# Three selected pages loaded early, turns woven with scores, and an output projection from three rounded products

## The chip, the cores and the metric

The kernel runs on one core of one Trainium2 chip, as one launch. The metric is the device time of that launch in microseconds (us), the median of several runs. The core's engines are TensorE (PE; its weight loads are listed as PEld), VectorE (DVE), ScalarE (ACT), GpSimd (POOL) and SyncE (SP, which issues most of the transfers). They run their own instruction streams and wait for each other through semaphores.

## The reference, cut to what matters

One inference step of one decoder layer, in float32, for a prompt of 1024 tokens and for 8 sample sequences of one token each with a past of 2048 tokens in pages of 128.

```python
h = x @ w_in                      # q | compressed k,v | selected k,v | window k,v | gates | HGRN2 parts | merge gates
a = NSA(h)                        # compressed blocks + selected top-16 blocks + sliding window, ALiBi
r = HGRN2(h)                      # gated linear recurrence
merged = sigmoid(g_a) * (a @ w_br_a) + sigmoid(g_r) * (r @ w_br_b)
mix = merged @ w_out              # (tokens, 1024) @ (1024, 1024): the output projection
x1 = LN(alpha * x + mix)
y = LN(alpha * x1 + relu(x1 @ w_up)**2 @ w_down)
```

For the sample sequences, the compressed branch turns all 16 pages of each sequence's `cache_cmp_kv` into block keys and values, and the selected branch attends to the 16 best of 33 blocks of `cache_sel_kv`:

```python
past_c = cache_cmp[page_table]                 # (8, 2048, 2, 2, 64)
kv_cmp = blocks_from_parts(chunk_parts(past_c, cmp_w), cmp_w, cmp_pos)
o_c, p_c = compressed_branch(q, pos_q, kv_cmp, slopes)
idx, valid = select_blocks(p_c, pos_q, n_sel)
o_s = selected_branch(q, pos_q, cache_sel[blocks idx], idx, valid, slopes)
```

## The kernel before

All orders are written out by hand: each engine has one program, and semaphores tie them together. Nearly all on-chip memory is one tensor, `arena`, that the phases cut up anew; `PS` is PSUM, eight banks of 512 floats. The phases follow each other: attention projections, prompt attention, sample attention (454 to 660 us of the profile), HGRN2 with its projections, merge, output projection with the first LayerNorm, then `up` and `down` of the MLP, and the second LayerNorm.

**Sample attention.** A "page" of this stage is a half: the 128 rows of 8 tokens that one half of each of a sequence's 16 pages gives, 1 MB in one indirect load by POOL (L2580), 128 partitions of 2048 floats. There are 16 for the compressed branch (n = 0 to 15) and 16 for the selected one (m = 0 to 15; sequence `m % 8`, half `m // 8`). Both use the two buffers of `raw` in turn. POOL issues load n when PE has turned load n-2 (`d_ps`), and from the third selected one on also when ACT has copied its values (`v_s`).

For a compressed page PE turns 16 blocks of 128x128 (`cmp_turn`, L1108), DVE and ACT copy them out of PSUM, and PE multiplies the previous page's by the compression weights (`cmp_products`, L1123). For a selected page m, `sel_turn` (L1147) turns the page's keys in two halves of four blocks, one PSUM bank each (4 and 5); ACT copies the values into `vall` (L1677) and then the first half of the turned keys into `ktd` (L1681), DVE copies the second half (L2152). `sel_scores` (L1156) multiplies the queries of the sequence by each half and adds up in banks 0 to 3. The two are called in turn: all of a page's turns, then all of its scores. `vall` has a place of 2048 floats for each sequence's values; those of sequences 5, 6 and 7 are first written by pages 5, 6 and 7. Between pages DVE also does the softmax of the compressed scores (L2096 on), the importance and rank of the blocks (L2110 to L2126), and after page 15 the maximum over the selected scores (L2141 on).

**Merge.** For 8 groups of 128 output channels and 3 chunks of 344 tokens, 24 steps s: PE makes two gates in split form and two plain products (L1407), ACT the sigmoids (L1764), DVE two products and their sum into `mT` (L2353, L2354), which frees the step (`m_dve2`).

**Split form.** Where the kernel calls `split_product` (L818), a float32 product is made from three products of rounded operands (`F32R`): high x high, high x low and low x high. The high part is a copy into an `F32R` tensor (ACT, L836 for weights), the low part is the value minus the high part (DVE, L842 for weights). A plain product of float32 operands shows as two records in the trace.

**Output projection.** `mT` holds the merged activations, 8 k-tiles of 128 channels x 1032 tokens; `wo` holds `w_out`, whose k-tiles 4 to 7 are loaded during the merge and 0 to 3 (L778) when the gates of the last step are done. PE goes through `LN_ORDER` = tile 0, the 8 sample rows (position p = 1), then tiles 1 to 7:

```python
for part in (1, 0):
    if p == 0:
        pe.wait_ge(wo_in[part], 16)
    for half in range(2):
        for k in range(4 * part, 4 * part + 4):
            mm = pe.matmul(PS[:, 2 * (p % 2) + half, :], mT[:, k, P * t:P * t + P],
                           wo[:, k, 512 * half:512 * (half + 1)], start=(k == 4), stop=(k == 3))
```

That is 16 plain products of 512 columns a tile (L1434). The sample rows take 16 products with 8 columns of weights, packed four at a time into strips of the array (L1440). After each tile DVE adds the residual (L2392, for the sample rows L2397 and L2402), takes the statistics and norms the tile (L2362 to L2369); PE turns the normed tile one position later (`turn_x1`, L1421), ACT copies the high part to `x1h` (L1809) and DVE makes the low part `xl` (L2378). `x1h` lies in the same place as `mT`. SP loads the two LayerNorm rows (L782, L783) and the residual rows (L788) behind eight `w_up` loads. `up` follows (L818 again), and then `down`, 512 columns a product, in split form.

## Time before, and what its profile page says

| what | us |
|---|---|
| median of the timed runs | 2204.72 |
| lowest and highest of the 3 | 2200.83, 2205.96 |
| the profiled execution | 2196.05 |
| its span, first to last instruction | 2194.2 |
| PE busy | 2118.1 |
| DVE busy | 1020.0 |
| ACT busy | 689.5 |
| POOL busy | 162.4 |

Busy times are the union of an engine's instructions in the profiled execution. The span is what the profile covers, and the execution's own time has a little around it. Matmuls are pipelined, so the duration of a record is longer than its distance from the next one; what a product costs is read from the distance. The mean granted PE clock is 0.99 of full speed.

### The profile page before, as it was taken

The numbers are of one execution on the slowest core, as the hardware profiler recorded it, in microseconds if no ns is written. First come the engines' busy times: TensorE is split into PE (matmuls) and PEld (weight loads), VectorE is DVE, ScalarE is ACT, GpSimd is POOL, SyncE is SP. The second block draws the span as 40 slices with busy tenths as digits, with TensorE's granted clock in tenths as the row PEclk, the third lists the DMA queues.
The fourth block names the chain that finished last, engine by engine and source line by source line (L and its number), as shares of the span: only waits on it lengthen the run. The fifth ranks groups of instructions, "written<-read, shape, count | busy, mean of one in ns | idle before, by whom it ended". The sixth has DMA issues, their size and how long they took to land.

```text
span 2194.2 us, 33354 instructions
## 1 busy us (share of the span) xinstructions
PE 2118.1 (97%) x14090; PEld 1800.0 (82%) x14090; DVE 1020.0 (46%) x1872; ACT 689.5 (31%) x1342; POOL 162.4 (7%) x164
## 2 busy tenths in 40 slices
PE   8999999989889999999999999999999999999997
PEld 8997777759659999999888884479888998889985
DVE  2136666636532666766212114544444444444447
ACT  3227777734432444544111110122211122111222
POOL 0030000001110221311000000000000000000007
PEclk9999999989999999999999999999999999999999
DMA  9322000146672221213212113021111111111101
GB/s 235 99 79 96 11 11 1 50 146 207 204 236 78 61 58 45 69 45 89 86 30 57 30 60 105 29 80 46 48 39 44 54 49 49 39 39 58 39 20 78
DMA packets 140625, 158.90 MB, mean 72 GB/s; under 512 B 25842, under 2 KB 122315, under 8 KB 135612
## 3 DMA queue, kind: packets, MB, share of 16 engines
q1 hardware_dynamic: 132444, 113.98, 17.3%
q0 software_dynamic: 8032, 42.78, 6.3%
q8 instruction: 112, 1.84, 0.3%
q14 instruction: 37, 0.30, 0.0%
HBM read 141.16 MB, written 19.76 MB: 73 GB/s over the span
## 4 chain that ended last, share of the span: by engine, by line
PE 90%; DVE 3%; DMA 3%; ACT 2%; issue 1%; SPq 0%; DVEq 0%; ACTq 0%; POOLq 0%
PE PS L818 58%; PE PS L1434 5%; PE PS L1407 5%; PE PS L1040 3%; PE PS L1123 3%; PE PS L1020 2%; DMA arena<-in_cache_sel_kv,arena 2%; PE PS L992 2%; PE PS L994 1%; PE PS L1108 1%; PE PS L1333 1%; PE PS L1476 1%; PE PS L1049 1%; PE PS L1276 1%; PE PS L1219 1%
## 5 line engine op out<-in xcount | busy, mean ns | idle before, releaser
L818 PE MATMUL PS<-x_low,w_high_mlp 128*128 128x344 f32 x1056 | 337.7, 320 | 0.0
L818 PE MATMUL PS<-w_down_high,hidden 128*128 128x512 f32 x960 | 308.1, 395 | 0.9 <-DVE w_down_low L2468 0.9
L818 PE MATMUL PS<-x_high,w_low 128*128 128x344 f32 x768 | 245.8, 320 | 0.0
L2462 DVE TENSOR_TENSOR arena<-arena,PS 128x512 f32<-128x512 f32 x244 | 167.5, 687 | 134.9 <-PE PS L818 134.7
L818 PE MATMUL PS<-x_high,w_high_mlp 128*128 128x344 f32 x720 | 229.8, 319 | 0.0
L818 PEld LDWEIGHTS PS<-w_down_high,hidden 128*128 128x128 f32 x960 | 180.1, 188 | 54.2 <-DVE arena L2462 12.0
L818 PE MATMUL PS<-w_down_low,hidden 128*128 128x512 f32 x512 | 201.0, 392 | 0.0
L818 PEld LDWEIGHTS PS<-x_low,w_high_mlp 128*128 128x128 f32 x1056 | 198.2, 188 | 2.5
L818 PE MATMUL PS<-x_low,w_high_hgrn 128*128 128x344 f32 x600 | 192.5, 321 | 0.0
L818 PE MATMUL PS<-x_high_a,w_low 128*128 128x344 f32 x480 | 154.1, 321 | 0.0
L818 PE MATMUL PS<-x_high_b,w_low 128*128 128x344 f32 x468 | 149.6, 320 | 0.0
L818 PEld LDWEIGHTS PS<-x_high,w_low 128*128 128x128 f32 x768 | 144.2, 188 | 0.0
L818 PEld LDWEIGHTS PS<-x_high,w_high_mlp 128*128 128x128 f32 x720 | 135.4, 188 | 1.5 <-issue 0.9
L1537 ACT ACTIVATE arena<-PS 128x344 f32<-128x344 f32 (+1 forms) x105 | 47.9, 458 | 262.6 <-PE PS L818 262.4
L1407 PE MATMUL PS<-arena,wring 128*128 128x344 f32 x384 | 114.7, 452 | 1.2 <-issue 1.2
L1836 ACT ACTIVATE w_down_high<-arena 128x2048 fp32r<-128x2048 f32 x15 | 28.7, 1916 | 275.2 <-PE PS L818 275.2
L1434 PE MATMUL PS<-arena 128*128 128x512 f32 x256 | 112.9, 599 | 1.8 <-DVE arena L2354 1.8
L818 PEld LDWEIGHTS PS<-x_low,w_high_hgrn 128*128 128x128 f32 x600 | 113.7, 189 | 0.0
L818 PEld LDWEIGHTS PS<-w_down_low,hidden 128*128 128x128 f32 x512 | 96.1, 188 | 21.2
L842 DVE TENSOR_TENSOR w_low<-wring,w_high_mlp 128x1024 fp32r<-128x1024 f32 x44 | 53.6, 1221 | 109.7 <-ACT w_high_mlp L836 109.7
L818 PE MATMUL PS<-x_high_a,w_high_hgrn 128*128 128x344 f32 x300 | 101.9, 340 | 1.5 <-DMA x_high_b<-x_high_kept 1.5
L2622 POOL TENSOR_TENSOR arena<-arena 128x1024 f32<-128x1024 f32 (+1 forms) x8 | 19.6, 2450 | 1119.1 <-ACT arena L1848 1119.1
(369 smaller groups left out, 4126.8 us busy)
## 6 DMA issues: line engine op xcount, KB each, us to landing
wring<-in_w_in SPq DMA_DIRECT2D x100, 256.0 KB, 3.4
wring<-in_w_up SPq DMA_DIRECT2D x64, 256.0 KB, 3.3
arena<-in_w_down SPq DMA_DIRECT2D x16, 1024.0 KB, 5.0
arena<-in_x_prompt SPq DMA_DIRECT2D x16, 512.0 KB, 3.8
x_high_kept<-x_high_att SPq DMA_DIRECT2D x1, 4128.0 KB, 14.3
arena<-in_cache_win_kv SPq DMA_DIRECT2D x8, 512.0 KB, 4.8
arena<-in_w_out SPq DMA_DIRECT2D x2, 2048.0 KB, 8.8
out<-in_cache_win_kv SPq DMA_DIRECT2D x1, 4088.0 KB
```

Of the source, the lines that this page charges most:

```text
L818: mm = pe.matmul(out, w, x, start=(start and k == 0 and i == 0), stop=(stop and k == tiles - 1 and i == 2))
L842: dve.tensor_tensor(wl[:, n % WR, :, 0:m], wring[:, n % WR, :, 0:m], high[:, :, 0:m].bitcast(F32), ALU.subtract).then_inc(wl_dve, 1)
L992: pe.matmul(out, qa, k1[g][:, br, k0:k0 + n], start=True, stop=False)
L994: mm = pe.matmul(out, qb, k2[br][g][0:65, k0:k0 + n], start=False, stop=True)
L1020: mm = pe.transpose(PS[0:n, 4 + turned % 2, P * b:P * (b + 1)], probs(j, col, n), ident)
L1040: mm = pe.matmul(PS[HD * two:HD * (two + 1), 6 + i % 2, c:c + P], v[0:r, :], PT[(2 * n + two) % 3][0:r, b // 4, P * (b % 4):P * (b % 4 + 1 ...
L1123: mm = pe.matmul(PS[:, 4 + 2 * (b % 2) + c, 0:256], cw2[:, c, 4 * half + q, :], xt2[:, n % 2, 256 * (4 * c + q):256 * (4 * c + q + 1)], st ...
L1407: mm = pe.matmul(PS[:, product_bank(s, ab), 0:cn], wring[:, n % WR, 4 * ab + k, :], a[:, k, c0:c0 + cn], start=(k == 0), stop=(k == 3))
L1434: mm = pe.matmul(PS[:, 2 * (p % 2) + half, :], mT[:, k, P * t:P * t + P], wo[:, k, 512 * half:512 * (half + 1)], start=(k == 4), stop=(k = ...
L1537: act.activation(dst[0:m, c0:c0 + cn], unit_out(3 * n + ci, m, cn), fn).then_inc(u_act, 1)
L1836: act.activation(wdh[:, :, :], wdn[:, g % 2], ACT.Copy).then_inc(wdh_act, 1)
L2462: dve.tensor_tensor(y, y, PS[:, 5 + d % 3, :], ALU.add).then_inc(dn_dve, 1)
```

## The change

1. **Loads.** The first three selected pages (`AHEAD = 3`) are loaded into the places of `vall` for sequences 5, 6 and 7, each issued right behind compressed page 4, 8 or 12. The other 13 use the two buffers of `raw` in turn, as before; the first two of them are issued when compressed pages 14 and 15 have been turned.
2. **Woven turns.** PE turns a half of page m+1, then multiplies the same half of page m, and so on.
3. **Projection.** Tiles 1 to 7 use the split form for k = 0 to 6 and a plain product for k = 7. Tile 0 uses the split form for k = 4, 5, 6 and plain products for the rest, and so do the sample rows. High parts of the activations go to `xl`, low parts over `mT` itself; high parts of the weights go to the room of the constants and of `aT`, low parts over `wo` itself. PE starts tile 0 before the last merge sum.

```diff
+        AHEAD = 3
+
+        def selected_raw(m):
+            if m < AHEAD:
+                b = NB - AHEAD + m
+                return vall[:, b, :, :].rearrange("p l c -> p (l c)")
+            return raw[:, (m - AHEAD) % 2, :]
+
+        def selected_in(m):
+            if m < AHEAD:
+                return ((kv_out[0], KV_ALL[0] + 16), (kv_out[1], KV_ALL[1] + 16), (vd_out, 16))[m]
+            return raw_in[(m - AHEAD) % 2], 16 * (8 + (m - AHEAD) // 2 + 1)
...
+        def out_high(k):
+            return wohK[:, k - 4] if k >= 4 else woha[:, k]
+        def mixed(p):
+            n = toks(LN_ORDER[p])
+            return (slice(None), slice(4, 7) if p < 2 else slice(0, 7), slice(P * LN_ORDER[p], P * LN_ORDER[p] + n))
...
# PE, selected pages
-            for m in range(16):
-                sel_turn(16 + m)
-                sel_scores(m)
+            for s in range(2):
+                sel_turn(0, s)
+            for m in range(16):
+                for s in range(2):
+                    if m + 1 < 16:
+                        sel_turn(m + 1, s)
+                    sel_scores(m, s)
...
# PE, projection
-            pe.wait_ge(m_dve2, NM)
+            pe.wait_ge(m_dve2, NM - 1)
...
+                pe.wait_ge(ul_dve, p + 1)
+                if p == 0:
+                    pe.wait_ge(wl_dve, SPLITS_O + 3)
+                    for half in range(2):
+                        for k in range(4, 7):
+                            split(PS[:, half, :], k, half, start=(k == 4))
+                        pe.matmul(PS[:, half, :], mT[:, 7, at], wo[:, 7, 512 * half:512 * (half + 1)], start=False, stop=False)
+                    pe.wait_ge(wo_in[0], 16)
+                    for half in range(2):
+                        for k in range(4):
+                            mm = pe.matmul(PS[:, half, :], mT[:, k, at], wo[:, k, 512 * half:512 * (half + 1)], start=False,
+                                           stop=(k == 3))
+                elif p == 1:
+                    pe.wait_ge(m_dve2, NM)
+                    for half in range(2):
+                        for k in range(4, 7):
+                            split(PS[0:NB, 2 + half, :], k, half, start=(k == 4), stop=(k == 6))
+                    for k in (0, 2, 7):
+                        for c in range(2 if k == 7 else 4):
...
+                else:
+                    for half in range(2):
+                        out = PS[:, 2 * (p % 2) + half, :]
+                        pe.matmul(out, mT[:, 7, at], wo[:, 7, 512 * half:512 * (half + 1)], start=True, stop=False)
+                        for k in (4, 5, 6, 0, 1, 2, 3):
+                            if p == 2 and half == 0 and k < 4:
+                                pe.wait_ge(wl_dve, SPLITS_O + 3 + k + 1)
+                            mm = split(out, k, half, stop=(k == 3))
...
# ACT
+                if s == NM - 4:
+                    act.wait_ge(wo_in[1], 16)
+                    for k in range(4, 7):
+                        act.activation(out_high(k), wo[:, k], ACT.Copy).then_inc(wh_act, 1)
...
+            mix_high(0)
+            mix_high(1)
+            act.wait_ge(m_dve2, NM)
+            for p in range(2, 4):
+                mix_high(p)
+            act.wait_ge(wo_in[0], 16)
+            for k in range(4):
+                act.activation(out_high(k), wo[:, k], ACT.Copy).then_inc(wh_act, 1)
+            for p in range(4, NQ + 1):
+                mix_high(p)
...
# DVE
+            def out_low(x, k):
+                dve.wait_ge(wh_act, SPLITS_O + x + 1)
+                dve.tensor_tensor(wol[:, k], wo[:, k], out_high(k).bitcast(F32), ALU.subtract).then_inc(wl_dve, 1)
+            def mix_low(p):
+                dve.wait_ge(uh_act, p + 1)
+                dve.wait_ge(m_dve2, NM if p else NM - 1)
+                dve.tensor_tensor(x1h[mixed(p)], mT[mixed(p)], xl[mixed(p)].bitcast(F32), ALU.subtract).then_inc(ul_dve, 1)
...
+                if s == NM - 3:
+                    for x, k in enumerate(range(4, 7)):
+                        out_low(x, k)
+                if s == NM - 1:
+                    mix_low(0)
...
+            for p in range(1, 4):
+                mix_low(p)
             dve.wait_ge(ln_in, 32)
             for p, t in enumerate(LN_ORDER):
                 dve.wait_ge(f_ps, p + 1)
+                if p == 1:
+                    for k in range(4):
+                        out_low(3 + k, k)
...
+                if 2 <= p <= NQ - 2:
+                    mix_low(p + 2)
...
# POOL
+            for n in range(16):
+                pool.wait_ge(d_ps, 2 * n + 6 if n < 2 else D_CMP + 4 * (n - 1))
+                pool.indirect_dma_start(out=raw[:, n % 2, :], out_offset=None, in_=cmp_rows, ...)
+                if n in (4, 8, 12):
+                    load_selected(n // 4 - 1)
+            for m in range(AHEAD, 16):
+                q = m - AHEAD
+                if q < 2:
+                    pool.wait_ge(d_ps, D_CMP + 4 * (15 + q))
+                else:
+                    pool.wait_ge(d_ps, D_SEL + 2 * (m - 1))
+                    pool.wait_ge(v_s, m - 1)
+                load_selected(m)
```

## Rows read from the trace of the kernel before

**Rows 1.** The page's busy times and shares of the span, all engines.
```profile
PE 2118.1 (97%) x14090; PEld 1800.0 (82%) x14090; DVE 1020.0 (46%) x1872; ACT 689.5 (31%) x1342; POOL 162.4 (7%) x164
```

**Rows 2.** Chain of waits, whole span: start us, us, what.
```profile
1309.04 4.64 PE PS L1407 x16
1315.43 14.01 PE PS L1434 x32
...
1352.46 13.93 PE PS L1434 x32
...
1425.70 13.73 PE PS L1434 x32
1440.31 11.35 PE PS L818 x72
```

**Rows 3.** Windows: length, busy us of PE, PEld, DVE, ACT, POOL, clock, DMA, GB/s.
```profile
1284.66:1296.84 12.18, 12.18 (x65) 10.59 (x65) 1.54 (x3) 0.92 (x2) 0.00 (x0) 1.00 0.00 1
...
1336.30:1340.00 3.70, 3.70 (x7) 1.72 (x6) 3.51 (x7) 1.23 (x3) 0.00 (x0) 0.57 0.25 35
...
1396.40:1411.00 14.60, 14.60 (x42) 6.90 (x42) 9.62 (x13) 3.15 (x6) 0.00 (x0) 1.00 0.11 37
...
538.00:570.00 32.00, 32.00 (x196) 28.91 (x195) 21.56 (x39) 16.00 (x27) 5.62 (x6) 1.00 0.62 204
604.00:624.00 20.00, 16.22 (x70) 7.17 (x68) 8.74 (x12) 7.96 (x10) 4.68 (x5) 1.00 0.85 280
```

**Rows 4.** Timeline around the sample rows' tile: start us, us, engine line.
```profile
1329.36 3.62 PE L1440 MATMUL PS<-arena 128*8 128x512 f32 x32
1329.53 1.22 DVE L2392 SCALAR_TENSOR_TENSOR arena<-arena,PS 128x1024 f32<-128x1024 f32 x1 [14.16 <-PE PS L1434]
...
1335.21 1.38 DVE L2397 SCALAR_TENSOR_TENSOR arena<-arena,PS 8x512 f32<-8x512 f32 x2
...
1335.35 1.35 PE L1421 MATMUL PS<-consts_sb,arena 128*128 128x128 f32 x8 [2.37 <-DVE arena L2369]
```

**Rows 5.** Two loads by line, each with its landing.
```profile
L778 SPq DMA_DIRECT2D arena<-in_w_out x1: 367/367/367, 1309.1 to 1309.1; - x1
...
DMA to landing us min/median/max: 8.2/8.2/8.2
...
L783 SPq DMA_DIRECT2D arena<-in_ln_b x1: 426/426/426, 1320.9 to 1320.9; - x1
...
DMA to landing us min/median/max: 6.1/6.1/6.1
```

**Rows 6.** PE's products of 512 columns in `down`, 1484 to 1497 us.
```profile
L818 PE MATMUL PS<-w_down_high,hidden x16: 391/392/397, 1490.5 to 1495.8; 128*128 128x512 f32 x16
...
L818 PE MATMUL PS<-w_down_low,hidden x8: 389/394/394, 1490.8 to 1495.6; 128*128 128x512 f32 x8
```

**Rows 7.** Chain of waits, 570 to 662 us.
```profile
579.67 1.76 PE PS L1165 x16
...
582.73 5.60 DMA arena<-in_cache_sel_kv,arena
...
608.95 1.11 PE PS L1147 x8
...
628.90 6.66 DMA arena<-in_cache_sel_kv,arena
...
637.18 1.94 PE PS L1156 x4
```

**Rows 8.** Timeline of POOL: one issue, with its idle time.
```profile
610.75 0.94 POOL L2580 DMA_INDIRECT arena<-in_cache_sel_kv,arena  x1 [3.72 <-PE PS L1147]
```

**Rows 9.** The 32 indirect loads of line 2580: issue to landing.
```profile
DMA to landing us min/median/max: 5.5/5.8/8.5
```

**Rows 10.** Copies and subtractions of one 128x1024 weight tile, by line.
```profile
L842 DVE TENSOR_TENSOR w_low<-wring,w_high_mlp 128x1024 fp32r<-128x1024 f32 x44 | 53.6, 1221 | 109.7 <-ACT w_high_mlp L836 109.7
L836 ACT ACTIVATE w_high_mlp<-wring 128x1024 fp32r<-128x1024 f32 x44 | 46.0, 1048 | 139.4 <-DMA wring<-in_w_in 139.4
```

More of the change, by code:

```diff
@@ L553, in hybrid_step @@
         wo = view(o, KD, D)
+        wol = rounded("w_out_low", arena_at, o, KD, D)
+        wohK = rounded("w_out_high_k", K_at, P, 3, D)
+        woha = rounded("w_out_high_a", aT_at, 0, 4, D)
+        assert P + 3 * D <= NC_
         wdn = view(o + 2 * KD * P, 2, 2, D)
@@ new lines, in _, with split @@
+                at = slice(P * t, P * t + toks(t))
+                def split(out, k, half, start=False, stop=False):
+                    cols = slice(512 * half, 512 * (half + 1))
+                    return split_product(pe, out, [xl[:, k, at]], [x1h[:, k, at]], [out_high(k)[:, cols]], [wol[:, k, cols]],
+                                         start=start, stop=stop)
+                if p == 0:
[16 more added lines that the diff above has]
+                        for c in range(2 if k == 7 else 4):
+                            j, half = c // 2, c % 2
+                            mm = pe.matmul(PS[32 * c:32 * c + NB, 2, :], mT[:, k + j, at],
+                                           wo[:, k + j, 512 * half:512 * (half + 1)], start=(k == 0 and c > 0),
+                                           stop=(k == (2 if j else 7)), skip_group_check=True)
+                else:
+                    for half in range(2):
[5 more added lines that the diff above has]
+                            mm = split(out, k, half, stop=(k == 3))
@@ L1675, in _ @@
                 b, half = selected(m)
[L1676 removed]
+                act.wait_ge(*selected_in(m))
                 act.activation(vall[:, b, 8 * half:8 * half + 8, :],
[L1678 removed]
+                               selected_raw(m).rearrange("p (l c) -> p l c", l=8)[:, :, P:2 * P], ACT.Copy).then_inc(v_s, 1)
                 act.wait_ge(d_ps, D_SEL + 2 * m + 1)
@@ L1788, in _, with mix_high @@
                     sigmoid(s, ab)
+            def mix_high(p):
+                act.activation(xl[mixed(p)], mT[mixed(p)], ACT.Copy).then_inc(uh_act, 1)
+            mix_high(0)
[8 more added lines that the diff above has]
+                mix_high(p)
             def deviation(p):
@@ L2401, in _ @@
                         y = x1[0:NB, NQ, 512 * half:512 * (half + 1)]
-                        ins = dve.tensor_tensor(y, y, PS[64 + 32 * half:64 + 32 * half + NB, 2 * (p % 2), :], ALU.add)
-                    ins.then_inc(f_dve, 1)
+                        lc(dve.tensor_tensor(y, y, PS[64 + 32 * half:64 + 32 * half + NB, 2 * (p % 2), :], ALU.add))
+                    y = x1[0:NB, NQ, 512:D]
+                    dve.tensor_tensor(y, y, PS[0:NB, 2 * (p % 2) + 1, :], ALU.add).then_inc(f_dve, 1)
                 dve.wait_ge(f_dve, p + 1)
```

78 lines of the change are left out of this document (30 added, 48 removed).

## The prediction

> **What bounds the kernel now.** I read the page's busy times first, then the chain of waits over the whole span, then the windows, the timeline and the chain of the two stages that the diff touches. TensorE (PE) is busy 97% of the span [rows 1]; whatever shortens the run has to take PE work or a PE wait away. The page's share alone does not say which, since the two stages are limited differently.
>
> *Output projection.* From 1315.43 to 1440.31 the chain of waits stays on PE: L1434, one prompt tile after another [rows 2]. A tile's 16 plain f32 products of 512 columns take 13.73 us, so 0.858 us a product; from the third tile's start (1352.46) to the first `up` product (1440.31) six tiles with their turns take 87.85 us, 14.64 each. In one such tile PE is busy 14.60 of 14.60 us while VectorE (DVE) works 9.62 and ScalarE (ACT) 3.15, and this is the tile with the extra weight splits [rows 3]. Here PE sets the pace, and fewer PE microseconds a tile are saved one for one, down to about 9.6 plus what DVE is given.
>
> *Selected pages.* From 604 to 624 PE is busy only 16.22 of 20.00 us, whereas in the compressed pages (538 to 570) it is busy 32.00 of 32.00 [rows 3]. The chain shows why: load, turn, load [rows 7]. Two buffers of one page each: page 3 lands at 588.33 and page 15 at 635.56, six links of two pages, 7.87 us a link. A landing to the next issue on the same buffer takes 1.80 us (608.95 to 610.75) [rows 7, 8], issue to landing 5.8 us in the middle and 5.5 at best [rows 9]. This stage is bound by latency, so PE work matters only where it lies inside the link.
>
> **The projection, step by step.** The added form is the one of the down stage: three rounded products of 512 columns with a 128x128 weight load each. There 24 of them start between 1490.5 and 1495.8, 23 steps, 0.230 us each [rows 6], so a split product costs 0.69 us against 0.858.
> 1. *Start.* Now PE ends the merge at 1313.68 and starts the projection at 1315.43, after DVE's last sum [rows 2]. After the change tile 0 needs only the sum before that one, and its low part: ACT copies three k-tiles (384 columns) before the last products end, DVE subtracts them in its idle time ahead of them. 1.75 us go. The weights' high and low parts for k = 4, 5, 6 (three copies of 1.05 and three subtractions of 1.22 us [rows 10]) lie in merge steps of 12.18 us, in each of which DVE works 1.54 and ACT 0.92 [rows 3]: nothing on the path. Without that cover they would cost 6.8 us once.
> 2. *Tile 0.* Six products in the split form, ten plain: 6 x 0.168 = 1.0 us less. Its second half needs `wo` 0 to 3, issued at 1309.1 and landed 8.2 us later, at 1317.3 [rows 5]; PE asks at 1319.5. Tile 0 ends at 1326.5 instead of 1329.4.
> 3. *The sample tile.* Now 16 packed plain products, four at a time, 3.62 us [rows 4]. After: 18 rounded products (4.14) and three rounds of packed ones (2.57), 6.7 us, ending at 1333.2. It gets 3.1 us *longer*, but PE now idles 2.37 us behind it until DVE has normed tile 0 (turn at 1335.35) [rows 4]. DVE's norm takes 5.8 us from 1329.53. After the change it cannot start at 1326.5, since it waits for the LayerNorm rows: issued 1320.9, landed 6.1 us later, 1327.0 [rows 5]; that transfer is late next. I put the norm at 1327.5, the turn at 1333.5: 1.85 us gained at this point (steps 1 to 3 together), and PE's idle time is filled.
> 4. *Tile 1.* Now it runs from 1336.3 to 1351.87, 15.5 us, because the granted clock is 0.57 for the first 3.7 us, behind the 2.37 us of idleness [rows 3, 4]. After, with no gap, 14 x 0.69 + 2 x 0.858 = 11.4 us. It must wait for the low parts of k = 0 to 3; DVE makes them from 1333.5 on, 1.25 us each; PE asks for the first at 1337.4, so hidden. But these 5 us stand on DVE ahead of the sample tile's residual (L2397 [rows 4]), and its norm (7.3 us now, plus one more add of 0.69) ends at about 1346.4 where PE asks at 1345.9: 0.5 us lost. 4.1 - 0.5 = 3.6 us gained.
> 5. *Six further tiles.* 14.64 becomes 11.38 + 0.88 (the turn) = 12.26: 6 x 2.35 = 14.0 us, with the difference of the plain and split products alone (14 x 0.168). DVE gets one subtraction of 896 columns a tile, 1.1 us: 10.7 us in the fullest tile, under 12.26. ACT's copies (nine of the mix, 0.95 us each, four weights, 4.2 us) run while PE does tile 0; ACT is free then.
>
> Sum: 1.85 + 3.6 + 14.0 = 19.4 us. Bounds: if DVE's two late points (the LayerNorm rows of step 3, the low parts ahead of the residual in step 4) cost 1.5 us more each, 16.4; if neither costs anything (norm at 1327.0, no wait in step 4), 20.4.
>
> **The pages, step by step.** Three selected pages (1 MB each) are issued behind compressed pages 4, 8, 12.
> 6. *Cost in the compressed stage.* PE is full there, the DMA engines are busy 0.62 [rows 3]; a compressed page is issued two pages (about 10 us) ahead and lands in 5.8, so it has about 2.7 us to spare. A further megabyte is about 3 us of the engines' time in a 5.3 us page with 2 us free: nothing on the path, 3 us in all at worst. POOL has 0.94 us more work and 4.3 us of idleness a page. The Trainium skill (DMA: Bandwidth & Descriptors, Queues, rings and completion order) says that each engine takes the descriptors of a ring in order; by that the extra page cannot hold up the compressed page issued before it, only the next, and the sum would keep the nothing I use. This trace has no such pair of loads.
> 7. *Gain in the selected stage.* Five pages are there at its start instead of two. But the chain then begins late: page 5 is issued when page 3 is turned. The compressed scores end at 581.4 as now [rows 7]; pages 1 and 2 follow at 2.6 to 3 us (turn halves 0.43 each, score halves 0.86), page 3 is turned at about 586.3, page 5 lands at 592.5.
> 8. *The link gets longer.* Woven turns put one scoring product (0.86) between the two halves of a turn, inside the link: landing to issue 1.72 + 0.5 = 2.3 us instead of 1.80. With 5.8 a link is 8.1 us; five links bring page 15 at 633.0 (now 635.56). Behind it two of page 14's products come first: 4.4 us to the end instead of 3.56, so 637.4 instead of 639.12 [rows 7]: **1.7 us gained**, of three pages' 11.8. Bounds: links at 7.5 with the shortest landings give 5.4 gained; landings of 6.66 as for page 15 [rows 7] in each link give 2.6 lost.
>
> The Trainium skill (DMA: Bandwidth & Descriptors, Anatomy of one DMA) prices such a load at 2.0 us plus bytes at 436 GB/s, 4.4 us for 1 MB; the sum by that would be an estimate of some 8 us more gain. The trace's 5.5 us at best disagrees, and decides.
>
> **Sum.** 19.4 + 1.7 = 21.1 us. The profiled execution took 2196.05 us around a span of 2194.2, 8.7 us under the median of the timed runs (2204.72, 2200.83 to 2205.96). I take the difference off both: 2175 for the next profiled one, **2183.6** for the median.
>
> **Rivals.**
> - *A, forecast:* both parts as worked. Within 4 us of 2183.6. Chance 0.62.
> - *B, the weave eats the early pages:* the longer link gives or takes nothing, or up to 2.6 us. Speaks for it that the link is already the bound and the weave lengthens just it; against, that five pages' start is three pages more. 2185.3 to 2187.9. Chance 0.20.
> - *C, more pages' gain:* landings are as short as 5.5 and copies hide; 5.4 instead of 1.7, 2179.9. Chance 0.08.
> - *D, the clock falls in the selected stage:* pages arrive in closer pairs, so PE's gap between pairs grows from about 2.4 to 2.9 us, and behind 2.37 us of idleness the clock did fall once [rows 3, 4], while the selected stage kept 1.00 [rows 3]. At 1.2 GHz a page's 2.6 us of PE work become 5.2, eleven pages 57 us instead of 45: 12 us lost, 2195.6. The Trainium skill (TensorE: Matmul & The Clock Gate, Loop structure matters more than you think) warns of just this, a wait for a DMA between short bursts of products. Chance 0.05.
> - *E, the split form is no cheaper here,* its weight loads or reads delayed by what DVE and ACT do beside it (0.286 a product): steps 2, 4 and 5 but for the clock's 1.8 us fall away, about 2200. The down stage does the same beside a busy DVE. Chance 0.03.
> - *F, slower:* the projection runs at the low clock. A tile at 1.2 GHz takes 22.8 us instead of 11.4; from two such tiles on (2 x 11.4 against 21.1) the change loses; all seven would give 2263. Against it: the projection has no gap over 1 us left, and its merge neighbours, as dense, run at 1.00. Chance 0.02.
>
> The range reaches from C's far side to B and the near part of D: 2177 to 2190; A's own is 2180 to 2188. A change of 0.2% (4.4 us) is about what a measurement of this kernel can tell from none. Faster by more than that: A to D and half of E, 0.96; within: 0.02; slower: F, 0.02.
>
> **What would show it.** In the profile after: L818 products in place of L1434 in the projection, tile period 12.2 to 12.3 us, first `up` product some 21 us earlier; no PE gap before the turn of tile 0 and no clock dip behind it; DVE waiting about 1 us for ln_b ahead of its first residual; POOL issuing selected pages at about 498, 519 and 540 with PE still full; a link of about 8.1 us, and landing to issue 2.3. Wrong would be: a tile period over 13, a link under 7.6 or over 8.8, PE idle in the compressed pages, or a clock under 1.00 after 584.

## The result and the profile after

The changed kernel takes **2190.86 us** (median of 6 runs, 2187.93 to 2196.18), the kernel before beside it 2205.34 (6 runs, 2200.83 to 2209.78): ratio 0.9937, 95% interval 0.9922 to 0.9951. It is 14.5 us faster. The forecast was 2183.6 with a range of 2177 to 2190, so the time lies 0.9 us above the range and 7.3 above the forecast.

The profiled execution took 2192.55 us with a span of 2190.7. The page's busy times, where before had [rows 1]:

```profile
PE 2116.0 (97%) x14200; PEld 1826.0 (83%) x14200; DVE 1035.0 (47%) x1889; ACT 703.7 (32%) x1358; POOL 162.3 (7%) x164
```

PE is 97% busy as before, and its busy time hardly moved. This row cannot tell where 14 us went; the stages can. In the table, a stage's length is taken between the same two instructions in every kernel; before was profiled a second time (2202.58 us, span 2200.8), and so was the changed kernel (2194.45 us, span 2192.6). Starts are read to 0.1 us, so a length in the third row can be 0.1 off.

| start or length, us | before | before, 2nd | after | after, 2nd |
|---|---|---|---|---|
| first turn of the compressed pages, at | 485.7 | 489.5 | 492.3 | 490.9 |
| first turn of the selected pages, at | 574.9 | 579.1 | 582.0 | 580.5 |
| selected stage: that turn to the start of the last score | 63.6 | 65.2 | 67.4 | 69.9 |
| projection: end of the last merge product to the first `up` product | 126.39 | 126.38 | 108.65 | 108.67 |

**The projection** gives 17.7 us, and gives the same in each profile. Windows of the changed kernel (columns as in [rows 3]): the stretch from the last merge product to the turn of tile 0, and one tile with its turn.

```profile
1326.40:1348.00 21.60, 19.72 (x77) 9.04 (x77) 9.53 (x14) 11.46 (x13) 0.00 (x0) 1.00 0.77 245
1399.00:1411.40 12.40, 12.40 (x56) 9.53 (x55) 10.69 (x14) 3.12 (x5) 0.00 (x0) 1.00 0.15 42
```

A tile takes 12.4 us of full PE where [rows 3] had 14.60, at clock 1.00. In the first window PE is busy 19.72 of 21.60 us: 1.9 us of idleness are left ahead of the turn of tile 0. The chain of waits in that stretch (start us, us, what) names the cause:

```profile
1321.77 4.64 PE PS L1439 x16
1326.41 0.24 SPq L706
...
1333.23 1.11 SPq L813
...
1334.39 0.42 SPq L814
...
1334.86 7.09 DMA arena<-in_x_prompt
...
1342.08 1.23 DVE arena L2484
...
1347.90 1.09 PE PS L1453 x8
1348.99 0.86 PE PS L1493 x2
```

The chain leaves PE for SyncE's queue. From 1322.2 on SyncE issues eight loads of `w_up` (L706), then the two LayerNorm rows (L813, L814), and only at 1334.86 the first x rows, which land at 1341.95. VectorE's residual (L2484) waits for them. Its timeline row has the length of the wait in brackets:

```profile
1342.08 1.22 DVE L2484 SCALAR_TENSOR_TENSOR arena<-arena,PS 128x1024 f32<-128x1024 f32 x1 [10.86 <-DMA arena<-in_x_prompt]
```

**The selected stage** became longer instead of shorter: by 3.8 us between the first profiles and by 4.7 between the second ones. First the early loads, in POOL's timeline; then the start of the stage, in windows; then one link of the chain, in the chain of waits (start us, us, what), to be compared with [rows 7, 8].

```profile
525.34 0.94 POOL L2676 DMA_INDIRECT arena<-in_cache_cmp_kv,arena  x1 [4.39 <-PE PS L1139]
526.58 0.94 POOL L2670 DMA_INDIRECT arena<-in_cache_sel_kv,arena  x1 [0.30 <-issue]
530.55 0.94 POOL L2676 DMA_INDIRECT arena<-in_cache_cmp_kv,arena  x1 [3.03 <-PE PS L1139]
```
```profile
505.00:560.00 55.00, 55.00 (x337) 49.59 (x335) 38.32 (x71) 26.89 (x46) 12.38 (x14) 1.00 0.73 253
...
581.90:585.90 4.00, 2.68 (x14) 1.78 (x15) 0.98 (x2) 2.61 (x3) 0.00 (x0) 0.81 0.00 0
585.90:589.90 4.00, 4.00 (x17) 1.99 (x16) 0.00 (x0) 0.60 (x1) 0.00 (x0) 0.76 0.00 0
589.90:593.90 4.00, 4.00 (x21) 1.96 (x19) 1.16 (x3) 2.35 (x5) 0.00 (x0) 1.00 0.00 0
```
```profile
596.51 5.84 DMA arena<-in_cache_sel_kv,arena
...
602.39 0.66 PE PS L1178 x4
603.05 1.00 PE PS L1184 x2
604.05 0.60 PE PS L1178 x4
604.65 0.26 issue
604.91 5.96 DMA arena<-in_cache_sel_kv,arena
...
638.87 5.94 DMA arena<-in_cache_sel_kv,arena
```

The early loads cost nothing: they are issued at 505.5, 526.6 and 547.7 and land 8.5 to 8.9 us later, and over this stretch PE is full, 55.00 of 55.00 us. From the first turn of the compressed pages to the first of the selected ones it is 89.2 and 89.7 us in the two profiles of before, 89.7 and 89.5 in those of the changed kernel. But page 5, the first load of the stage, is issued at 596.51, 14.6 us after the first turn, and a link now reads: landing, half a turn 0.66, one page's score half 1.00, the other half of the turn 0.60, 0.26 to the issue. That is 2.56 us from landing to issue, and five links from 596.51 to 638.87 are 8.47 us each, where before had 7.70 over its six, counted in the same way from issue to issue.

### The profile page after: what moved, and what is told of

It is laid out like the page before. It is cut to its first block, busy times and chain, and to the rows that moved or that the text cites. A ratio compares the mean times of both kernels' runs of the same rounds, so it can differ in the third digit from the quotient of the medians.

```text
span 2190.7 us, 33621 instructions
## 1 busy us (share of the span) xinstructions
PE 2116.0 (97%) x14200; PEld 1826.0 (83%) x14200; DVE 1035.0 (47%) x1889; ACT 703.7 (32%) x1358; POOL 162.3 (7%) x164
## 3 DMA queue, kind: packets, MB, share of 16 engines
q8 instruction: 113, 1.85, 0.3%
## 4 chain that ended last, share of the span: by engine, by line
PE 90%; DMA 3%; DVE 3%; ACT 2%; issue 1%; SPq 0%; DVEq 0%; ACTq 0%; POOLq 0%
PE PS L849 62%; PE PS L1439 5%; PE PS L1071 3%; PE PS L1051 3%; PE PS L1154 3%; DMA arena<-in_cache_sel_kv,arena 2%; PE PS L1023 2%; PE PS L1025 1%; PE PS L1139 1%; PE PS L1365 1%; PE PS L1531 1%; PE PS L1080 1%; DMA arena<-in_x_prompt 1%; PE PS L1184 1%; PE PS L1251 1%
## 5 line engine op out<-in xcount | busy, mean ns | idle before, releaser
L1439 PEld LDWEIGHTS PS<-arena,wring 128*128 128x128 f32 x384 | 72.1, 190 | 35.1 <-issue 1.4
```

Source lines behind the costliest of these rows:

```text
L1439: mm = pe.matmul(PS[:, product_bank(s, ab), 0:cn], wring[:, n % WR, 4 * ab + k, :], a[:, k, c0:c0 + cn], start=(k == 0), stop=(k == 3))
```

## The experiments

Each is the changed kernel with the edit shown, except that experiment 8 is an edit of experiment 7's kernel and experiment 9 of experiment 8's. "Flat" is the order of turns and scores of the kernel before:

```diff
-            for s in range(2):
-                sel_turn(0, s)
             for m in range(16):
                 for s in range(2):
-                    if m + 1 < 16:
-                        sel_turn(m + 1, s)
-                    sel_scores(m, s)
+                    sel_turn(m, s)
+                for s in range(2):
+                    sel_scores(m, s)
```

The theory at this point: the projection gives some 18 us whatever the pages do, and the selected stage is bound by the link, which the weave lengthened. The rival: the early loads or the clock cost the time.

**1. The projection alone** (flat, `AHEAD = 0`).

> The changed kernel with the selected stage of before: no early pages, both halves of a page turned and then scored. Stage length is counted from the first turn of selected page 0 to the end of the last scoring product: 64.2 us before, 68.1 after. Theory 1 (the weave lengthens the load link and costs more than the early pages bring): stage 64.2 +- 1 us, projection as in the changed kernel (from the last merge product to the first up product 108.9 us, before 126.6), total about 16.9 us under before, so faster than the whole change by about 3.9 us. Rival (the selected stage's 3.9 us are a chance of one execution): total about 2191, no better than the whole change.

2190.56 us (4 runs, 2188.94 to 2194.36), ratio 0.9933, 0.9916 to 0.9950: as fast as the whole change. The selected stage takes 64.1 us, as in before, where the changed kernel has 67.4 and 69.9. The 3.9 us that were expected of the time do not show in it; the interval is almost 4 us wide to either side, so the time decides nothing here and the stage does. The two edits of the pages together bring no gain.

**2. Early pages, flat turns.**

> The changed kernel with the three early pages but without the weave. Theory 1: landing to next issue falls back from 2.56 to about 1.8 us and a link from 8.47 to about 7.9 us; page 5 is issued some 14 us into the stage, so the stage takes about 63.0 us, 5 less than with the weave and 1.2 less than before; total about 18 us under before. Rival (the early pages themselves cost, by DMA contention or by the low clock at the start of the stage, and the weave is neutral): stage 66 to 68 us.

2187.69 us (2185.35 to 2190.51), ratio 0.9918, 0.9902 to 0.9935. The stage takes 63.1 us, its links 8.02. That is 1.0 us less than in experiment 1, and little more than chance: the three flat profiles with early pages (this one, experiment 5 and the flat one of experiment 10) have 63.1, 64.1 and 63.5 us, the three without (before twice, experiment 1) 63.6, 65.2 and 64.1.

**3. The weave without early pages** (`AHEAD = 0`).

> The changed kernel with the weave but no early pages. Theory 1: page 3 is issued about 6 us into the stage and lands at 12, six links of 8.47 and 5.2 us behind the last landing give 68 to 69 us, some 4 to 5 over before; total about 12 us under before. Rival (the weave is neutral): stage 64.2 us, total about 17 under before.

2194.84 us (2186.66 to 2198.30), ratio 0.9934, 0.9910 to 0.9958. The ratio is that of experiment 1, though the medians are 4.3 us apart: here too the stage has to tell. It takes 72.7 us in the profiled run (2198.30 us, the slowest of the four), more than expected: its links average 9.25, and the granted clock falls in it. PE's timeline and a window over the same microseconds:

```profile
597.53 0.59 PE L1184 MATMUL PS<-arena 128*64 128x512 f32 x1
600.26 1.07 PE L1178 MATMUL PS<-consts_sb,arena 128*128 128x128 f32 x4 [2.14 <-DMA arena<-in_cache_sel_kv,arena]
601.26 1.97 PE L1184 MATMUL PS<-arena 128*64 128x512 f32 x2
```
```profile
600.00:604.00 4.00, 3.74 (x10) 1.65 (x10) 0.00 (x0) 1.73 (x3) 0.00 (x0) 0.57 0.55 227
```

Behind 2.14 us of waiting for a page the half turn takes 1.07 instead of 0.66 and the score half's two records 1.97 instead of 1.07, at clock 0.57, near the lower of the two levels (1.2 of 2.4 GHz). The Trainium skill (TensorE: Matmul & The Clock Gate, Loop structure matters more than you think) says that a long DMA wait between products lets PE go cold; this row agrees. In the first profile of the changed kernel PE's waits for the later pages are 0.16 to 1.66 us, and the clock stays at 1.00. The length of one wait does not decide it: in experiment 2 the clock falls (0.76 and 0.81 in two windows of 4 us) behind a wait of 1.51 us.

The four kernels make a square of stage lengths: flat 64.1 without and 63.1 with early pages, woven 72.7 without and 67.4 with. The weave costs 4.3 us with early pages. The other profiles bear it out: the three woven ones with early pages have 67.4, 69.9 and 68.5 us (the changed kernel twice, experiment 10), all above the flat 63.1 to 64.1.

**4. Early pages, page m+1 turned whole ahead of both scores of m.** This takes the score out of the middle of the turn.

```diff
                 for s in range(2):
                     if m + 1 < 16:
                         sel_turn(m + 1, s)
+                for s in range(2):
                     sel_scores(m, s)
```

> The changed kernel with early pages, and page m+1 turned whole before both halves of page m are scored. The scoring product leaves the link but stays behind it. Theory 1 in its exact form (what costs is the scoring product between the two halves of a turn): landing to issue about 1.8 us, links of 7.9, and 5.2 us behind the last landing as with the weave: stage 64 to 65 us. If instead any reordering of turns and scores costs (switching between the two kinds of products), the stage stays at 67 to 68.

2189.27 us (2185.90 to 2193.93), ratio 0.9924, 0.9902 to 0.9945. The stage takes 69.3 us, not 64 to 65: a miss. Landing to issue is 1.8 us again where nothing else is late (609.95 to 611.76), but PE then waited 3.28 us for a page, and the clock fell behind it:

```profile
613.30 1.11 PE L1178 MATMUL PS<-consts_sb,arena 128*128 128x128 f32 x8 [0.18 <-DMA arena<-in_cache_sel_kv,arena]
614.34 1.93 PE L1184 MATMUL PS<-arena 128*64 128x512 f32 x4
619.55 1.97 PE L1178 MATMUL PS<-consts_sb,arena 128*128 128x128 f32 x8 [3.28 <-DMA arena<-in_cache_sel_kv,arena]
```

The first link, at clock 1.00, is 9.20 us for another reason. The order made PE wait for VectorE's copy of the page before, which stood behind the importance steps:

```profile
602.75 0.66 PE L1178 MATMUL PS<-consts_sb,arena 128*128 128x128 f32 x4 [1.97 <-DVE arena L2226]
```

The same eight turns take 1.11 us before the wait of 3.28 and 1.97 behind it. So this run shows the shorter way from landing to issue, but not what it would be worth: VectorE's copy and the clock took it back, and of the two theories it decides neither.

**5. The x rows first** (flat turns, early pages, and SyncE's order).

```diff
-            for n in range(U_U, U_U + WR):
+            for n in range(U_U, U_U + 2):
                 load_unit(n)
...
             for p, t in enumerate(LN_ORDER):
+                if p == 2:
+                    for n in range(U_U + 2, U_U + WR):
+                        load_unit(n)
```

> Flat turns and three early pages, and SyncE issues the two LayerNorm rows and the first two x rows after two of the four w_up units instead of after all four. Theory (late rows): in the projection VectorE's residual sum of tile 0 waited for an x tile that was queued behind eight w_up loads (10.98 us) and the ln rows; with four loads fewer ahead, the rows land some 4 to 5 us earlier (1337 where the changed kernel had 1341.95, against a first product of 1326.4), the idle time before the residual sum falls from 10.86 to 6 us or less, tile 0 is normed before the sample tile's packed products end, and PE's gap before its turn, about 1.7 us, goes: the projection takes 107.2 where it took 108.9 and the run 2185.8 where the same kernel without this order took 2187.7. Rival (bandwidth): the rows come as late as before, because the six other transfers share the same engines, and the projection stays 108.9. Second rival: the two w_up units that now come later are late for the up stage, which then starts late or stalls by some us.

2186.50 us (2182.60 to 2190.59), ratio 0.9908, 0.9885 to 0.9930. The projection takes 106.92 us instead of 108.55 in experiment 2: 1.6 us, as expected (the medians, 1.2 apart, cannot show so little). The residual of tile 0 now waits for PE, in VectorE's timeline:

```profile
1335.04 1.22 DVE L2485 SCALAR_TENSOR_TENSOR arena<-arena,PS 128x1024 f32<-128x1024 f32 x1 [8.04 <-PE PS L1478]
```

It starts 12.9 us after the last merge product, where the changed kernel's started 15.7 after it, and the turn of tile 0 comes 19.55 us after that product instead of 21.5.

**6. Before and the changed kernel once more**, for a second profile of each.

> The kernel before once more, for a second profile. If the 7 us by which the changed kernel is later at the start of the compressed pages (485.7 in the profile before, 491 to 494 in all five changed ones) belong to the one execution that was profiled, this one starts them at 491 to 494 too. If they come from the change, it starts them near 485.7 again. The selected stage should again take 63.5 to 64.5 us and the projection 126 to 127.

> The changed kernel once more, for a second profile. If its clock in the selected stage is a matter of the execution, the stage takes something between 65 and 73 us, with two-level dips of the granted clock where the four woven variants so far showed them (16 to 20, 40 to 44, 68 to 72 us of the stage); if the length is set by longer links alone it is again 67 to 68.5 us, with links of 8.3 to 8.6. The projection should again take 108.5 to 109.5.

The figures stand in the table above. The compressed pages start at 489.5 in the second profile of before, between the two cases that were expected. So part of the 6.6 us by which the changed kernel was late there belongs to the executions. PE's last product ahead of that start ends at 481.3 and 484.4 in before, at 484.8 and 484.5 in the changed kernel; then PE waits for the first compressed page, 4.4 and 5.0 us in before, 7.5 and 6.4 in the changed kernel, with the same code. Whether the change has a part in this wait stays open. The woven stage is 69.9 us with links of 8.54.

**7. Four buffers.** If the stage is bound by load latency, more buffers must free it; if by PE or the copies, they do nothing. Pages 0 to 4 are loaded ahead into places of `vall`, pages 5 and 6 into the space of `aT`, which is empty by then and serves as two more buffers (`SLOT` 2 and 3). The load of `xa`, which overwrites that space, moves behind page 10.

```diff
+        AHEAD = 5
+        SLOT = {5: 2, 6: 3, 7: 0, 8: 1, 9: 2, 10: 3, 11: 0, 12: 1, 13: 0, 14: 1, 15: 0}
+        FREED_BY = {9: 5, 10: 6, 11: 7, 12: 8, 13: 11, 14: 12, 15: 13}
+        EARLY = [2, 4, 6, 8, 10, 12, 14]
...
+                    pool.wait_ge(d_ps, D_SEL + 2 * (FREED_BY[m] + 1))
+                    pool.wait_ge(v_s, FREED_BY[m] + 1)
```

> Flat turns; five selected pages are loaded ahead into places of later values, two more into space of the prompt's kept rows, which serves as two more page buffers (the load of x_high's first half moves from the compressed pages to behind selected page 10); SyncE's order as in the run above. Theory (latency): the selected pages are bound by turn, issue, landing of 8.0 to 8.5 us for two pages; with four buffers a page is due 12 us after its issue, lands in time, and the stage is bound by PE's own work, 8 turns (1.3 us) and two products (2 x 0.86) a page, 3.1 to 3.3 us: 16 pages take 51 to 54 us instead of 63.1 (first turn to last score), and the run takes 2175 to 2178. Rival (pace of the copies): a page takes 3.9 us because ACT's copy of the values (1.06) and the two copies of the turned keys lie in the chain, whatever is loaded: the stage stays at 62 to 63 and the run at 2186. Second rival: the later load of x_high (2 MB) is late for the products behind the stage, and up to 6 us of the gain are lost there.

2179.93 us (2176.40 to 2187.62), ratio 0.9886, 0.9859 to 0.9914. The time is near the expected one, but the stage is not: 65.6 us in the profile, where experiment 5 had 64.1. The execution that was profiled (2176.80 us) owes its time to what lies ahead, with the compressed pages starting at 483.9 instead of 490.8. Neither theory nor rival had this. Of these 6.9 us, 4.8 are PE's wait for the first compressed page. SyncE's queue and PE in experiment 5, then PE here:

```profile
477.62 0.58 SPq L772 DMA_DIRECT2D x_high_a<-x_high_kept  x1
490.80 5.56 PE L1142 MATMUL PS<-consts_sb,arena 128*128 128x128 f32 x28 [6.39 <-DMA arena<-in_cache_cmp_kv,arena]
```
```profile
483.94 1.97 PE L1151 MATMUL PS<-consts_sb,arena 128*128 128x128 f32 x16 [1.56 <-DMA arena<-in_cache_cmp_kv,arena]
```

In experiment 5 the 2 MB load of `xa` goes out 2.6 us ahead of that page, and PE can turn the page only 10.6 us after its issue; here `xa` is loaded later, and it is 5.7 us. So this edit has a second effect besides the buffers. It comes again in experiments 8 and 9 (waits of 1.51 and 2.38 us, against 4.4 to 7.5 in all eleven profiles with two buffers), but no run moves that load alone. The chain of waits shows what the selected stage itself met:

```profile
588.47 0.33 PE PS L1211 x2
...
597.48 0.18 DVE arena L2207
...
597.68 8.14 DMA arena<-in_dbias
...
605.92 2.30 DVE arena L2218
...
608.24 0.70 DVE arena L2235
...
608.98 1.07 PE PS L1196 x2
...
619.58 7.44 DMA arena<-in_cache_sel_kv,arena
```

Pages 1 to 7 run at 3.2 us each. Then PE waits 3.63 us for VectorE's copy of the turned keys (L2235), which stands behind the block mask (L2218), which waits for the bias rows. SyncE may load these only when VectorE has finished the block ranks (L2207), since the ranks lie in the same place; that load takes 8.14 us. In the kernels before, pages came so slowly that it was nearly hidden. Behind it, page 13 had to wait for page 11 to be turned, and its load (7.44 us) is in the chain again.

**8. The mask later.** The edit moves the mask behind page 10 and lets page 10, not 11, free the place for page 13. The steps that follow the mask move with it, and `xa` is loaded in two parts, the first behind page 9.

```diff
-        SLOT = {5: 2, 6: 3, 7: 0, 8: 1, 9: 2, 10: 3, 11: 0, 12: 1, 13: 0, 14: 1, 15: 0}
-        FREED_BY = {9: 5, 10: 6, 11: 7, 12: 8, 13: 11, 14: 12, 15: 13}
+        SLOT = {5: 2, 6: 3, 7: 0, 8: 1, 9: 2, 10: 3, 11: 0, 12: 1, 13: 3, 14: 0, 15: 1}
+        FREED_BY = {9: 5, 10: 6, 11: 7, 12: 8, 13: 10, 14: 11, 15: 12}
...
-                if m == 7:
+                if m == 10:
                     block_mask()
```

> The four-buffer kernel (flat turns) with two edits. VectorE's block mask moves from behind page 7 to behind page 10, and the steps that follow it likewise (scores of the first half added behind page 11, window turned behind 14), because the mask waited for the bias rows, 8.14 us of load that SyncE may issue only once the block ranks are done; and the ring of buffers gives page 13 a place that page 10 frees instead of one that page 11 frees (14 after 11, 15 after 12), x_high's first half being loaded in two parts. Theory (the stall was the bias load, then the ring's last pages): pages 0 to 7 ran at 3.22 us each in the run before; now all sixteen do, 51.5 us, with 2.6 us of other products among them: first turn to last score 54 to 56 us instead of 65.6, and the run 2168 to 2171 against 2179.9. Rival (VectorE is late anyway): the importance, tie and rank steps, 1.2 to 1.3 us each behind a copy of 0.69, already filled VectorE, and the mask (2.3 us) delays the copy of the next page wherever it stands: the stage keeps 3 to 5 us of stall, 59 to 61. Second rival: the second part of x_high (1 MB), issued some 8 us before the stage ends, is late, and up to 3 us are lost ahead of the products behind the stage.

2174.94 us (2169.36 to 2182.10), ratio 0.9871, 0.9843 to 0.9899. The stage takes 58.1 us, between the two expectations. PE's timeline, for pages 9 and 10 (start us, us):

```profile
607.01 1.10 PE L1193 MATMUL PS<-consts_sb,aT 128*128 128x128 f32 x8
608.35 1.93 PE L1199 MATMUL PS<-arena 128*64 128x512 f32 x4 [0.25 <-ACT arena L1749]
610.22 1.09 PE L1193 MATMUL PS<-consts_sb,aT 128*128 128x128 f32 x8
```

From 579.65 on every page takes 3.2 us, with 0.25 of idleness in it. One wait is 0.65 us, a few other products stand between the pages, and no page is waited for. The 2 to 4 us above the expectation lie in the first 8 us: page 0 and the compressed scores run at clock 0.59 in this execution, 8.35 us where the run before needed 5.96. VectorE's lateness, the rival, costs 0.4 us. The later load of x_high is waited for nowhere.

**9. Four buffers and the weave.**

> As the kernel beside it, but with the woven turns of the change instead of the flat ones. Theory (the weave costs through the link: it puts a score half of 1.00 us and both turn halves between a landing and the next issue): with four buffers the link is hidden, so the weave costs nothing here, and the stage takes within 1 us of its flat twin, since a woven page is two turn halves of about 0.6 and two score halves of 1.00, 3.2 us, and a flat page is 3.22. Rival (the weave makes PE's own work longer, or ties it closer to VectorE, whose copy of page m+1 stands behind its long steps of page m only in the flat order): the stage is 3 us or more longer than its flat twin, as it was with two buffers (67.4 against 63.1).

2173.66 us (2170.51 to 2176.55), ratio 0.9854, 0.9829 to 0.9879. The stage takes 57.4 us, 0.7 less than its flat twin. The weave that costs 4 us with two buffers costs nothing with four. This kernel is the fastest of all here; against its flat twin the 1.3 us between the medians decide nothing. The two are 11.6 and 12.8 us below experiment 5, their stages 6.0 and 6.7 us shorter. Most of the rest lies ahead of the stage in the profiles: PE waits 4.9 and 4.0 us less for the first compressed page (experiment 7), and the compressed pages take 88.3 and 88.4 us instead of 90.0. By this estimate four buffers are worth some 6 to 8 us of the 12. Ranges of 6 to 13 us over four runs leave the sum unsure.

**10. Woven and flat side by side**, five rounds, both with the x rows first.

> The changed kernel with one edit: SyncE issues the LayerNorm rows and the first two x rows after two of the four w_up units. Woven turns, two buffers, three early pages as in the change. Both theories expect the projection 1.7 us shorter than in the changed kernel (106.9 us from the last merge product to the first up product, as in the flat kernel with this order, against 108.65). Theory (link): the woven stage is again 67 to 70 us from first turn to last score, links of 8.4 to 8.6 and page 15's issue to the end 10 to 12, so that the run is 2188 to 2190 and 2.5 to 5 us above its flat twin beside it. Rival (the difference between woven and flat seen so far was the spread of executions): over five rounds the two are within 1.5 us of each other.

> The flat twin, run once before over three rounds (2186.5 us): flat turns, three early pages, two buffers, the same SyncE order. Theory (link): first turn to last score 62.5 to 65 us, links of 8.0 to 8.2, page 15's issue to the end 8.8 to 9.5; the run 2184 to 2187, 2.5 to 5 us below the woven kernel beside it. Rival (spread of executions): within 1.5 us of it.

Woven 2191.20 us (2182.79 to 2193.38), ratio 0.9948, 0.9934 to 0.9962; flat 2185.94 (2183.20 to 2189.71), ratio 0.9930, 0.9917 to 0.9943. The medians are 5.3 us apart, the stages of the profiles 68.5 and 63.5 us, the links 8.66 and 8.16. The ranges overlap, and so do the ends of the two intervals; stage and link show what the medians only suggest. The projection is 106.92 and 106.91 us: the order of the rows does the same under both. It was expected to bring the woven kernel to 2188 to 2190; the median did not show it.

## Why the prediction was wrong, step by step

The projection sets the gain, as forecast, and the weave lengthens the link, as forecast. But the forecast had the selected stage 1.7 us shorter, and it became 3.8 longer. The sizes were off by 1.7 us in the projection and by 5.5 in the selected stage; their sum, 7.2, is close to the 7.3 between forecast and median, closer than medians with intervals of 3 us to either side allow one to claim. What failed most is step 7 with step 8.

- *Step 7, the start of the chain.* The step put the issue of page 5 (its landing less 5.8) 11.8 us after the first turn; it was 14.6 and 15.3 us in the two profiles. 2.4 of the 2.8 us lie in one term: the compressed scores were to end 6.5 us after the first turn, as in before, and ended 8.9 after it. In windows from the first turn to that end, in before, in the changed kernel and in experiment 3 (woven too):

```profile
574.94:581.36 6.42, 6.03 (x29) 3.96 (x28) 0.98 (x2) 2.60 (x3) 0.94 (x1) 0.74 0.37 112
```
```profile
581.95:590.81 8.86, 7.54 (x38) 4.45 (x37) 0.98 (x2) 3.21 (x4) 0.00 (x0) 0.81 0.00 0
```
```profile
583.84:591.17 7.33, 6.01 (x37) 3.83 (x36) 0.98 (x2) 3.20 (x4) 1.87 (x2) 1.00 0.44 154
```

  The weave puts the turn of page 1 ahead of the compressed scores, and the step left it behind them: 7.33 us at clock 1.00 is already 0.9 more than before took with part of its stretch at the lower clock. The other 1.5 us are the clock of this execution. The rest are the pages behind: one whose data are there was put at 2.6 to 3 us, from turn halves of 0.43 and score halves of 0.86, less than half of the whole ones in [rows 7] (1.11 and 1.94); alternating they measure 0.60 and 1.00, 3.2 us a page.
- *Step 8, the link.* Predicted 2.3 us from landing to issue and 8.1 a link, measured 2.56 and 8.47: the 0.26 are the same two halves, the rest are landings of 5.9 on the mean. Five links, 1.9 us. The tail behind the last landing is 5.2 us instead of 4.4.
- *What steps 7 and 8 missed in kind:* the three early pages were set at 11.8 us, of which 1.7 were to be left. They never had that much to give, because a flat page at its quickest takes 3.2 us and a page within the links 3.8 to 4.1. A page taken out of the links is worth the difference, 0.6 to 0.9 us, so some 2 us for three. In the profile of experiment 2 page 5 is issued 1.8 us earlier than in experiment 1; longer links and a longer tail took half of it back, and the single profiles scatter by as much.
- *Step 6* was right: PE is full with all three early loads inside, 5.2 us a page as before. The order of descriptors that step 6 takes from the Trainium skill (DMA: Bandwidth & Descriptors, Queues, rings and completion order), by which the early load can delay only the compressed page behind it, agrees with the landings in experiment 2: the compressed pages issued just ahead of an early load land in 5.46, 5.79 and 5.58 us, those just behind it in 8.56, 7.11 and 7.97.
- *Steps 1 and 2* were right: the residual of tile 0 could start 12.9 us after the last merge product (experiment 5), where the step says 12.8.
- *Step 3* named the wrong late transfer. It had the LayerNorm rows land last, at 1327.0. But the x rows stand behind them on SyncE's queue, and in before they landed 6.9 us after their issue, at 1328.3, 0.8 us behind the step's norm; there PE was later still, and nothing waited:

```profile
1321.39 0.43 SPq L788 DMA_DIRECT2D arena<-in_x_prompt  x1
```

  In the changed kernel they are issued 8.5 us after the last merge product instead of 7.7 and take 7.1, so that the residual starts 15.7 us after it, where the step has 13.8. The 1.85 us of the step came out as 0.2; experiment 5 gave 1.6 of them back by the order alone.
- *Steps 4 and 5* hold: tile 1 takes 11.48 us at clock 1.00 (predicted 11.4) and gains 4.1; six tiles take 12.375 each (predicted 12.26), 13.6 us instead of 14.0. (By the step's own 14.64 and 12.26 it would be 14.3; the 14.0 leave out what the turn was to gain.)
- *The rivals.* B is what happened in kind, but by more than its worst case, 2187.9: no rival had the measured time. Of the prediction's own signs of being wrong one was met, a clock under 1.00 after 584; tile period, link and PE in the compressed pages stayed inside theirs. D's condition was met in experiments 3 and 4, where the clock did fall behind waits of 2.1 to 3.3 us; in the first profile of the changed kernel it stayed at 1.00 from 589.9 on. The chance of 0.05 for it was low, and the fall is no matter of the weave alone: behind the first 8 us of the stage the clock falls in four of the five woven or turn-first profiles with two buffers (the second of the changed kernel, experiments 3, 4 and 10), in all three flat ones with early pages (experiments 2, 5 and 10), and in none of the three flat ones without (before twice, experiment 1). The falls are short, and none costs the 12 us of D. E, F and C are ruled out by the window of 12.40 us at 1.00 and by the links.

Open is how much of the difference between the woven and the flat stage is the link and how much the clock in any one execution. In the profiles, by terms: page 5 is issued 0.9 us later in the changed kernel than in experiment 2 (14.6 against 13.7 us after the first turn), five links are 0.45 longer each, and page 15's issue to the last score is 10.5 instead of 9.4. That is 4.3 us, all of the difference of 67.4 and 63.1. But the clock, 0.97 on the mean over the stage in both, falls in different places: at the start in the changed kernel, where it costs 1.5 us (step 7), and in the middle, within the links, in experiment 2. What is free of it are links at clock 1.00: 8.47 on the mean for the five of the changed kernel, 7.70 for the six of before, 7.88 for the six of experiment 1. The link is some 0.6 to 0.8 us longer by the weave; the rest of the difference in any pair is not separated.

## What to carry to other kernels

Where a stage is a ring of load, use and reissue, count what a page costs inside the ring and outside it: prefetching some pages is worth only the difference, and an order that fills PE but stands between a landing and the next issue makes every link longer. Give the ring more buffers first; then the order hardly matters, and the next wait (here the bias rows behind the ranks) shows itself. Look also at what an edit moves elsewhere: 4 to 5 of the 12 us by which the four-buffer kernels gained came, by the profiles, with a load that no longer stood ahead of the first page. When a step starts earlier, follow every transfer that it waits for along the queue that feeds it, not only the one that seemed last in the old profile.

## What the runs showed of the hardware

- *Two levels of the clock, by the execution.* The same code takes almost 9 us more in one execution than in another: PE's last product ahead of the first compressed page ends at 481.0 in the woven kernel of experiment 10 and at 489.6 in experiment 3. Windows of the changed kernel and of experiment 8 over the same stretch:

```profile
160.00:200.00 40.00, 38.28 (x261) 30.23 (x259) 25.30 (x54) 25.34 (x84) 9.42 (x14) 0.79 0.42 152
```
```profile
160.00:200.00 40.00, 37.84 (x277) 29.31 (x276) 26.03 (x59) 26.12 (x87) 7.92 (x11) 0.87 0.42 149
```

  The granted clock is 0.79 in one and 0.87 in the other, and that last product ends at 484.8 and 481.6. (The compressed pages start at 492.3 and 483.1; the other 6 us between these are the wait for the first page.) The two first profiles, of before and of the changed kernel, are only 3.5 us apart where the medians are 14.5 apart; the lengths of single stages are steadier (126.39 and 126.38, 108.65 and 108.67).
- *Loads beside loads.* Behind a 2 MB load issued 2.6 us ahead of it, the first compressed page (1 MB) can be turned 8.6 to 11.7 us after its issue (eleven profiles); without that load 5.7 to 6.5 us after (experiments 7, 8 and 9). The bias rows (64 x 2048 floats), with page loads beside them in every kernel, take 5.6 to 8.7 us over the fourteen profiles.
